# Four changed k pairs instead of three in the first feed-forward, and one k pair's low halves made by ScalarE and an accumulating DMA

## The chip, the core and the metric

The kernel runs on one core of one Trainium2 chip. The time is the device time of one execution in microseconds (us), the median of several runs. The engines of the core work side by side and wait for each other by semaphores: PE (TensorE, matrix products), PEld (its weight loads), DVE (VectorE), ACT (ScalarE), POOL (GpSimd) and SP (SyncE, which issues most of the transfers here). Transfers from HBM run on 16 shared DMA engines.

## The reference, cut to what is touched

The program computes two transformer blocks on 256 tokens of width 2048, in float32. The change is in the first block's feed-forward:

```
hn = rmsnorm(h, ffn_norm[l])                                  # 256 x 2048
h = h + (silu(hn @ w_gate[l]) * (hn @ w_up[l])) @ w_down[l]   # w_gate, w_up: 2048 x 5632
```

The two products hn @ w_gate and hn @ w_up are the ones whose schedule changes. What is computed stays as it is.

## The kernel before, in words

**Split operands.** A float32 operand is used as two parts, hi (the value rounded to the narrower matmul form, called F32R here) and lo (value minus hi). A product of two such operands is three matmuls: hi x hi, hi x lo, lo x hi (`product`, lines 1005 to 1007 are its three matmuls).

**Tiles and pairs.** The 5632 columns of w_gate and w_up are cut into 11 strips of 512 (W). A strip of w_gate and the same strip of w_up form one pair, f0 to f10 (`run_b[2:13]`); `ffn_b` is f1 to f10. The contraction over 2048 rows is cut into eight k pairs, 0 to 7. Each k pair has two chunks of 2 x 128 rows x 512 columns (512 KB): h = 0 from w_gate, h = 1 from w_up. Below, (k, h) is a chunk, so (7, 0) is k pair 7's chunk of w_gate.

**Plain and changed k pairs.** In a plain k pair (`plain_pair`) each chunk needs 4 products, so a k pair is 8 products or 24 matmuls. In a changed k pair (`strassen`, the Strassen-Winograd scheme on 2 x 2 blocks) it is 7 products or 21 matmuls. For that, DVE adds up four new tiles of 128 x 512 (`sums`, lines 2430, 2431, 2434, 2436): three go to the tile tf (sums T1, T2 and T4), the fourth replaces part of chunk h = 1 in place (T3). ACT makes their hi parts (`t_hi_of`, line 1608) and DVE their lo parts (`t_lo_of`, line 2450). tf has two sets in turn, so the sums of a changed k pair wait until PE is through with the changed k pair before the last one. Which k pairs are changed stands in the tuple F_S = (0, 3, 5). f0 has none (E_S).

**The activations' side.** A changed k pair also needs four combinations of the blocks of hn. They are built once, while f0 runs, for all later pairs: `x_forms` (DVE, lines 2401 to 2408/2409), `x_form_hi` (ACT, line 1580) and `x_form_lo` (DVE, line 2414). Those of the feed-forward are in xf, three places.

**A chunk's way.** There are six places for chunks (wf; wf_raw is the same memory read as plain float32; the second half of a place holds first the raw chunk and then its lo part). The k-th chunk takes the place of the chunk six before it. SP (`pair_chunks`, line 653) waits until PE has counted that chunk as used (f_used) and issues the load. Then ACT makes hi (`f_hi_of`, line 1601), then DVE makes lo in place (`f_lo_of`, line 2443), and PE waits for lo by the counter f_lo. In a changed k pair PE counts chunk 0 used after 6 matmuls and chunk 1 after 12, since it multiplies with the b21 and b22 parts early; only in k pair 0, where the result banks are still being read, it does that "late", after 15 and 18 matmuls.

**What sets the order.** Every engine's order is written out by hand. Within a pair f_n, ACT takes: the gates of the pair before (`gates_on`, line 1615), the hi parts and t_hi as listed, `p1_copy` (line 1651: copies one PSUM bank after the last changed k pair, k = 5, is done), the first three chunks and t_hi(0) of the next pair, `ff_copy`, and (1, 1) and (2, 0) of the next pair. DVE takes lo(1, 1), lo(2, 0), `gated_up` of the pair before (line 2505), lo(2, 1), the changed k pair 3, lo(4, 0), lo(4, 1), the changed k pair 5, the lo parts of k pairs 6 and 7, `middle` (lines 2465, 2467, 2468: combines PSUM banks, waits for p1_copy), and `to_next`: the first two sums of the next pair's k pair 0, `middle_end` (line 2473, counts y_ok), the other two sums, lo(0, 0), lo(0, 1), lo(1, 0), t_lo(0), then `finish` and `finish_up` (lines 2485, 2486, 2498), which read the result banks when PE is through with k pair 7. Ahead of k pair 7 PE waits for y_ok and turns the finished strip of the pair before (8 transposes, line 694).

**POOL** does nothing between its load of hres at 428 us and the one of gfbc at 1302 us.

Of the kernel before, what the change touches and what calls it, by code (L numbers as in the profile page):

```python
# [29 lines left out]
ALU = mybir.AluOpType  # L30
# [68 lines left out]
F_S = (0, 3, 5)  # L99
# [116 lines left out]
def two_blocks(nc, a, out):  # L216
    ctx = ExitStack()
    with ctx:
# [157 lines left out]
        t1_ok, t2_ok, t3_ok, t4_ok = sem("t1_ok"), sem("t2_ok"), sem("t3_ok"), sem("t4_ok")  # L376
        t_hi, t_lo, t_used = sem("t_hi"), sem("t_lo"), sem("t_used")
# [309 lines left out]
        def _(pe):  # L687
# [357 lines left out]
            def forms(p, k):  # L1045

                if p.wide:
                    return [[x_place(p.stage, F_S.index(k))[0][:, j, f, :] for j in range(2)] for f in range(4)]
                if p.run:
                    place = AGAIN_PLACE if p is e1 and k in E_AGAIN else D_S2.index(k)  # L1050
                    return [[ef4[:, place, j, f, :] for j in range(2)] for f in range(4)]
                return [operand(p, 2 * k, 1)] + [[ef[:, D_S.index(k), j, f, :] for j in range(2)] for f in range(3)]

            def strassen(p, k, begun):
# [12 lines left out]
                pe.wait_ge(f_lo, ca + 1)  # L1067
# [273 lines left out]
        def _(act):  # L1341
# [251 lines left out]
            def f_hi_of(p, k, h):  # L1593
# [497 lines left out]
        def _(dve):  # L2091
# [1093 lines left out]
        def _(pool):  # L3185
# [66 lines left out]

            pool.wait_ge(f_used, F_END)
# [57 lines left out]
```

## Time and profile before

| | us |
|---|---|
| median of 3 runs | 2432.6 (2431.69 to 2432.75) |
| span of the profiled execution | 2429.9 |
| PE busy in it | 2417.6 |
| DVE busy | 1881.4 |
| ACT busy | 1387.7 |
| POOL busy | 50.6 |

The span is the time from the first to the last instruction of one profiled execution; the run time also has what lies around it, 2.7 us by the median. PE's clock was granted in full except at the edges (mean 0.999). The pairs f1 to f10 lie between 643.8 and 1068.0 us of the span. The transfers' engines were busy 61 to 66% of the time. A row of the timeline gives an instruction's start, its duration, its engine, line and operands; matmul durations overlap, so their cost is the distance between starts.

### The profile page before, as it was taken

Reading aid. Unit: us, or ns where it says so; the run is one execution under the profiler, and the core shown is the slowest. Engines: PE = TensorE matmul, PEld = TensorE weight load, DVE = VectorE, ACT = ScalarE, POOL = GpSimd, SP = SyncE. Lnnn points to the kernel's source line nnn. Section 1 sums busy time; section 2 is a strip of 40 time slices with the busy share of each in tenths; the row PEclk is TensorE's granted clock in tenths of the full one; section 3 lists DMA queues with packets and bytes.
Section 4 is the critical chain, followed back from the end, with each engine's and each line's share of the span. In section 5 each row is a group of like instructions: output and inputs, shape, how many; then the busy total and the mean of one; then the engine's idle time right before and its main releaser. Section 6 shows DMA issues by size and latency. Waiting matters only on the chain.

```text
span 2429.9 us, 29002 instructions
## 1 busy us (share of the span) xinstructions
PE 2417.6 (99%) x11145; PEld 2008.2 (83%) x11145; DVE 1881.4 (77%) x2411; ACT 1387.7 (57%) x1744; POOL 50.6 (2%) x93
## 2 busy tenths in 40 slices
PE   9999999999999999999999999999999999999998
PEld 7888888888888888888888888888788888888887
DVE  6455555688898888989777587664889999999877
ACT  6446555445655555556456464564666666666554
POOL 1000110000000000000001100000000000000000
PEclk9999999999999999999999999999999999999999
DMA  7655555666666666666666555566566666666675
GB/s 238 198 172 155 185 156 162 217 192 191 191 197 200 201 195 203 195 192 202 197 208 198 167 154 161 155 191 197 167 197 193 196 200 188 194 195 189 200 215 169
DMA packets 239299, 460.11 MB, mean 189 GB/s; under 512 B 16582, under 2 KB 18800, under 8 KB 238528
## 3 DMA queue, kind: packets, MB, share of 16 engines
q1 hardware_dynamic: 237760, 452.65, 61.2%
q0 software_dynamic: 1376, 5.69, 0.7%
q8 instruction: 85, 1.39, 0.2%
q14 instruction: 46, 0.38, 0.1%
q10 hardware_dynamic: 32, 0.01, 0.0%
HBM read 456.19 MB, written 2.10 MB: 189 GB/s over the span
## 4 chain that ended last, share of the span: by engine, by line
PE 98%; DVE 1%; DMA 0%; SPq 0%; issue 0%; ACT 0%; DVEq 0%; ACTq 0%
PE acc L1005 16%; PE acc L1007 16%; PE acc L1006 16%; PE acc L721 11%; PE acc L723 11%; PE acc L722 11%; PE mis L1006 3%; PE mis L1005 3%; PE mis L1007 3%; PE mis L694 1%; PE mis L1290 1%; PE mis L819 1%; PE mis L1199 1%; PE acc L740 1%; PE acc L741 1%; PE acc L742 1%
## 5 line engine op out<-in xcount | busy, mean ns | idle before, releaser
L1601 ACT ACTIVATE wf<-wf_raw 128x1024 fp32r<-128x1024 f32 x544 | 568.4, 1058 | 548.3 <-DVE wf_raw L2431 219.1
L2443 DVE TENSOR_TENSOR wf<-wf_raw,wf 128x1024 fp32r<-128x1024 f32 x544 | 643.3, 1219 | 79.1 <-ACT wf L1601 75.6
L2099 DVE TENSOR_TENSOR lo<-raw,hi 128x1024 fp32r<-128x1024 f32 (+1 forms) x313 | 376.5, 1219 | 231.1 <-ACT hi L1354 228.7
L1354 ACT ACTIVATE hi<-raw 128x1024 fp32r<-128x1024 f32 (+1 forms) x313 | 321.0, 1049 | 162.9 <-PE acc L723 139.0
L1005 PE MATMUL acc<-wf,xb_hi 128*128 128x512 f32 x931 | 365.3, 392 | 0.0
L1007 PE MATMUL acc<-wf,xb_lo 128*128 128x512 f32 x931 | 362.7, 390 | 0.0
L1006 PE MATMUL acc<-wf,xb_hi 128*128 128x512 f32 x931 | 362.3, 389 | 0.0
L721 PE MATMUL acc<-hi,xa_hi 128*128 128x512 f32 (+1 forms) x576 | 224.4, 390 | 0.0
L723 PE MATMUL acc<-hi,xa_lo 128*128 128x512 f32 (+1 forms) x576 | 221.8, 385 | 0.0
L722 PE MATMUL acc<-lo,xa_hi 128*128 128x512 f32 (+1 forms) x576 | 221.6, 385 | 0.0
L721 PE MATMUL acc<-hi,xb_hi 128*128 128x512 f32 x544 | 216.4, 398 | 0.0
L723 PE MATMUL acc<-hi,xb_lo 128*128 128x512 f32 x544 | 212.2, 390 | 0.0
L722 PE MATMUL acc<-lo,xb_hi 128*128 128x512 f32 x544 | 211.9, 389 | 0.0
L1005 PE MATMUL acc<-wf,ff_top_hi 128*128 128x512 f32 x543 | 211.5, 390 | 0.0
L1007 PE MATMUL acc<-wf,ff_in_place_lo 128*128 128x512 f32 x543 | 211.3, 389 | 0.0
L1006 PE MATMUL acc<-wf,ff_top_hi 128*128 128x512 f32 x543 | 211.2, 389 | 0.0
L1007 PEld LDWEIGHTS acc<-wf,xb_lo 128*128 128x128 f32 x931 | 174.8, 188 | 36.6
L1005 PEld LDWEIGHTS acc<-wf,xb_hi 128*128 128x128 f32 x931 | 174.8, 188 | 35.7 <-DVE wf L2443 0.6
L1006 PEld LDWEIGHTS acc<-wf,xb_hi 128*128 128x128 f32 x931 | 174.9, 188 | 35.3
L723 PEld LDWEIGHTS acc<-hi,xa_lo 128*128 128x128 f32 x576 | 108.1, 188 | 21.5
L721 PEld LDWEIGHTS acc<-hi,xa_hi 128*128 128x128 f32 x576 | 108.2, 188 | 20.4
L722 PEld LDWEIGHTS acc<-lo,xa_hi 128*128 128x128 f32 x576 | 108.3, 188 | 20.3
(530 smaller groups left out, 3800.0 us busy)
## 6 DMA issues: line engine op xcount, KB each, us to landing
raw<-in_w_in SPq DMA_DIRECT2D x215, 512.0 KB, 4.2
wf_raw<-in_w_ffn_in SPq DMA_DIRECT2D x160, 512.0 KB, 3.7
wf_raw<-in_w_gate SPq DMA_DIRECT2D x88, 512.0 KB, 3.7
wf_raw<-in_w_up SPq DMA_DIRECT2D x88, 512.0 KB, 3.8
wf_raw<-in_w_down SPq DMA_DIRECT2D x88, 512.0 KB, 4.5
wf_raw<-in_w_ffn_out SPq DMA_DIRECT2D x88, 512.0 KB, 4.0
wf_raw<-in_w_out SPq DMA_DIRECT2D x32, 512.0 KB, 4.5
raw<-in_w_o SPq DMA_DIRECT2D x32, 512.0 KB, 4.9
```

What stands on the lines that cost most here:

```text
L694: last = nc.tensor.transpose(mis[pair][:, kb, t * P:(t + 1) * P], src[:, t, kb * P:(kb + 1) * P], ident[:, :])
L721: nc.tensor.matmul(o, xh, wh, start=kb == 0, stop=False)
L722: nc.tensor.matmul(o, xh, wl, start=False, stop=False)
L723: last = nc.tensor.matmul(o, xl, wh, start=False, stop=kb == k - 1)
L740: nc.tensor.matmul(o, xh, wh, start=kb == 0, stop=False)
L1005: nc.tensor.matmul(o, x[0], wh, start=first, stop=False)
L1006: nc.tensor.matmul(o, x[0], wl, start=False, stop=False)
L1007: return nc.tensor.matmul(o, x[1], wh, start=False, stop=end)
L1354: nc.scalar.activation(hi[:, slot, :, 0:width], raw[:, slot, :, 0:width], ACT.Copy)\
L1601: nc.scalar.activation(wf[:, f_slot[c], 0, :, :], wf_raw[:, f_slot[c], 1, :, :], ACT.Copy)\
L2099: V.tensor_tensor(lo[:, slot, :, 0:width], raw[:, slot, :, 0:width], hi[:, slot, :, 0:width].bitcast(F32), ALU.subtract).then_inc(lo_ready, 1)
L2443: V.tensor_tensor(wf[:, f_slot[c], 1, :, :], wf_raw[:, f_slot[c], 1, :, :], wf[:, f_slot[c], 0, :, :].bitcast(F32), ALU.subtract).then_inc ...
```

## The change

The table of changed k pairs becomes one table for each stage; the first feed-forward now has (0, 2, 4, 5) in place of (0, 3, 5), the other stages stay as they are. With four of them, a fourth combination of hn is built during f0, in the place xo, which the stage before has used. For k pair 7 of f1 to f10, DVE no longer makes the lo parts: ACT makes hi and then writes minus hi over it from the raw chunk, in place of the raw chunk; a DMA issued by POOL then loads the same chunk from HBM again and adds it to minus hi, which leaves lo. PE waits for that DMA (lo_in) instead of f_lo. POOL waits for minus_hi before each.

```diff
-F_S = (0, 3, 5)
+S_K = dict(out=(0, 3, 5), ffn=(0, 2, 4, 5), ffn2=(0, 3, 5))
+S_AT = dict(out=(3, 1, 2), ffn=(0, 3, 1, 2), ffn2=(0, 1, 2))
...
+N_K = 7
...
+        def by_dma(p, k):
+
+            return p in ffn_b and k == N_K
+
+        def lo_made(p, k, h):
+
+            c = p.chunk(k, h)
+            if by_dma(p, k):
+                return lo_in[h], 16 * (ffn_b.index(p) + 1)
+            return f_lo, c + 1 - sum(q.chunk(N_K, j) < c for q in ffn_b for j in range(2))
...
                 nc.scalar.activation(wf[:, f_slot[c], 0, :, :], wf_raw[:, f_slot[c], 1, :, :], ACT.Copy)\
                     .then_inc(f_hi, 1)
+                if by_dma(p, k):
+                    act.wait_ge(f_hi, c + 1)
+                    nc.scalar.activation(wf[:, f_slot[c], 1, :, :], wf_raw[:, f_slot[c], 1, :, :], ACT.Copy, scale=-1.0)\
+                        .then_inc(minus_hi, 1)
...
@@ ACT, f0
             f_hi_of(f0, 7, 0)
+            x_form_hi("ffn", 3)
             f_hi_of(f0, 7, 1)
@@ ACT, every pair of ffn_b
                 f_hi_of(p, 2, 1)
                 f_hi_of(p, 3, 0)
+                t_hi_of(p, 2)
                 f_hi_of(p, 3, 1)
                 f_hi_of(p, 4, 0)
-                t_hi_of(p, 3)
                 f_hi_of(p, 4, 1)
                 f_hi_of(p, 5, 0)
+                t_hi_of(p, 4)
                 f_hi_of(p, 5, 1)
                 f_hi_of(p, 6, 0)
                 t_hi_of(p, 5)
@@ DVE, f0
             x_form_lo("ffn", 2)
+            x_forms("ffn", 3)
             f_lo_of(f0, 7, 0)
             f_lo_of(f0, 7, 1)
+            x_form_lo("ffn", 3)
@@ DVE, every pair of ffn_b
                 f_lo_of(p, 1, 1)
-                f_lo_of(p, 2, 0)
+                strassen(p, 2)
                 gated_up(run_b[p.no - 1])
-                f_lo_of(p, 2, 1)
-                strassen(p, 3)
-                f_lo_of(p, 4, 0)
-                f_lo_of(p, 4, 1)
+                f_lo_of(p, 3, 0)
+                f_lo_of(p, 3, 1)
+                strassen(p, 4)
                 strassen(p, 5)
-                for k in (6, 7):
-                    f_lo_of(p, k, 0)
-                    f_lo_of(p, k, 1)
+                f_lo_of(p, 6, 0)
+                f_lo_of(p, 6, 1)
                 middle(p)
@@ POOL
+            for i, p in enumerate(ffn_b):
+                for h in range(2):
+                    c = p.chunk(N_K, h)
+                    pool.wait_ge(minus_hi, 2 * i + h + 1)
+                    if i:
+                        pool.wait_ge(lo_in[h], 16 * i)
+                    pool.dma_start(wf[:, f_slot[c], 1, :, :],
+                                   (w_gate, w_up)[h][:, CK * N_K:CK * N_K + CK, p.i * W:(p.i + 1) * W],
+                                   accum_op=ALU.add).then_inc(lo_in[h], 16)
```

ACT, pair f10, from the gates on, before. wf<-wf_raw is a hi part (f_in4 and the like name the place of its chunk: here (2, 1), (3, 0), (3, 1), (4, 0), then (4, 1)), tf<-tf_raw is t_hi.

```order
L1615 ACTIVATE dsum<-dsum,small 128x512
L1601 ACTIVATE wf<-wf_raw 128x1024 [waits f_in4]
L1601 ACTIVATE wf<-wf_raw 128x1024 [waits f_in1]
L1601 ACTIVATE wf<-wf_raw 128x1024 [waits t3_ok,f_in0]
L1601 ACTIVATE wf<-wf_raw 128x1024 [waits f_in3]
L1608 ACTIVATE tf<-tf_raw 128x1536 [waits t4_ok]
L1601 ACTIVATE wf<-wf_raw 128x1024 [waits f_in5]
```

The same place now, where the lines have moved (1601 is 1616, 1608 is 1627, 1615 is 1634):

```order
L1634 ACTIVATE dsum<-dsum,small 128x512
L1616 ACTIVATE wf<-wf_raw 128x1024 [waits t3_ok,f_in4]
L1616 ACTIVATE wf<-wf_raw 128x1024 [waits f_in1]
L1627 ACTIVATE tf<-tf_raw 128x1536 [waits t4_ok]
L1616 ACTIVATE wf<-wf_raw 128x1024 [waits f_in0]
L1616 ACTIVATE wf<-wf_raw 128x1024 [waits f_in3]
L1616 ACTIVATE wf<-wf_raw 128x1024 [waits t3_ok,f_in5]
```

The first t_hi of a pair is now that of k pair 2 and stands right behind hi(3, 0), whose chunk is loaded to place 1; in the form before, the first one belonged to k pair 3 and stood behind hi(4, 0).

ACT at the end of the same pair, before: t_hi(5), hi(6, 1), hi(7, 0), hi(7, 1), p1_copy.

```order
L1608 ACTIVATE tf<-tf_raw 128x1536 [waits t4_ok]
L1601 ACTIVATE wf<-wf_raw 128x1024 [waits f_in0]
L1601 ACTIVATE wf<-wf_raw 128x1024 [waits f_in3]
L1601 ACTIVATE wf<-wf_raw 128x1024 [waits f_in5]
L1651 ACTIVATE dsum<-mis 128x512 [waits staged,t_used]
```

And now:

```order
L1627 ACTIVATE tf<-tf_raw 128x1536 [waits t4_ok]
L1616 ACTIVATE wf<-wf_raw 128x1024 [waits f_in0]
L1616 ACTIVATE wf<-wf_raw 128x1024 [waits f_in3]
L1620 ACTIVATE wf<-wf_raw 128x1024 [waits f_hi]
L1616 ACTIVATE wf<-wf_raw 128x1024 [waits f_in5]
L1620 ACTIVATE wf<-wf_raw 128x1024 [waits f_hi]
L1670 ACTIVATE dsum<-mis 128x512 [waits staged,t_used]
```

Two more ACT instructions stand ahead of p1_copy, each behind a wait for the one before it.

DVE at the end of f0, before: lo(6, 1), the third x_form_lo, lo(7, 0) and lo(7, 1), then the first sum of f1.

```order
L2443 TENSOR_TENSOR wf<-wf_raw,wf 128x1024 [waits f_hi]
L2414 TENSOR_TENSOR xf<-xf_raw,xf 128x512 [waits xf_hi]
L2443 TENSOR_TENSOR wf<-wf_raw,wf 128x1024 [waits f_hi] x2
L2640 ISA x4
L2430 TENSOR_TENSOR tf_raw<-wf_raw 128x512 [waits t_used,f_in0,f_in1]
```

And now (2443 is 2464, 2414 is 2435, 2430 is 2451, 2401 to 2409 are 2422 to 2430):

```order
L2464 TENSOR_TENSOR wf<-wf_raw,wf 128x1024 [waits f_hi]
L2435 TENSOR_TENSOR xf<-xf_raw,xf 128x512 [waits xf_hi]
L2422 TENSOR_TENSOR usum<-xb_hi,xb_lo 128x512 [waits xf_sum]
L2427 TENSOR_TENSOR xf_raw<-usum 128x128 [waits dve_chain]
L2428 TENSOR_TENSOR xf_raw<-usum 128x128
L2429 TENSOR_TENSOR xf_raw<-usum,xf_raw 128x128 [waits dve_chain]
L2430 TENSOR_TENSOR xf_raw<-usum,xf_raw 128x128 [waits dve_chain]
L2464 TENSOR_TENSOR wf<-wf_raw,wf 128x1024 [waits f_hi] x2
L2435 TENSOR_TENSOR xf<-xf_raw,xf 128x512 [waits xf_hi]
L2663 ISA x4
L2451 TENSOR_TENSOR tf_raw<-wf_raw 128x512 [waits t_used,f_in0,f_in1]
```

Six instructions more stand between lo(6, 1) and the sums of f1.

## Rows read from the trace of the kernel before

**Rows 1.** The page: its head and its busy times by engine
```profile
span 2429.9 us, 29002 instructions
...
PE 2417.6 (99%) x11145; PEld 2008.2 (83%) x11145; DVE 1881.4 (77%) x2411; ACT 1387.7 (57%) x1744; POOL 50.6 (2%) x93
```

**Rows 2.** Table by stretches: one pair's period; busy us by engine, clock, DMA
```profile
949.60:991.90 42.30, 42.30 (x192) 35.12 (x192) 37.48 (x41) 23.68 (x24) 0.00 (x0) 1.00 0.65 199
```

**Rows 3.** Waits between 640 and 1080 us: total us, times, longest
```profile
PEld acc L1005 <- DVE usum L2495: 0.4, 1, 0.4
```

**Rows 4.** Timeline of PE in f8 and f9: start, us, what
```profile
966.65 0.39 PE L1005 MATMUL mis<-wf,xb_hi 128*128 128x512 f32 x1
...
976.86 1.04 PE L694 MATMUL mis<-ident,stg 128*128 128x128 f32 x8
...
983.18 0.39 PE L1005 MATMUL mis<-wf,xb_hi 128*128 128x512 f32 x1
```

**Rows 5.** Timeline of SP's queue, then the landing of the load at 969.6
```profile
969.56 0.37 SPq L653 DMA_DIRECT2D wf_raw<-in_w_up  x1
...
986.78 0.37 SPq L653 DMA_DIRECT2D wf_raw<-in_w_gate  x1
...
DMA to landing us min/median/max: 4.9/4.9/4.9
```

**Rows 6.** Timeline of ACT in f8 and f9, idle time before in brackets
```profile
965.26 1.04 ACT L1601 ACTIVATE wf<-wf_raw 128x1024 fp32r<-128x1024 f32 x1
...
971.61 0.60 ACT L1651 ACTIVATE dsum<-mis 128x512 f32<-128x512 f32 x1
...
990.56 1.06 ACT L1601 ACTIVATE wf<-wf_raw 128x1024 fp32r<-128x1024 f32 x1 [2.37 <-DMA wf_raw<-in_w_gate]
...
994.55 1.06 ACT L1601 ACTIVATE wf<-wf_raw 128x1024 fp32r<-128x1024 f32 x1 [0.19 <-DMA wf_raw<-in_w_gate]
995.52 1.47 ACT L1608 ACTIVATE tf<-tf_raw 128x1536 fp32r<-128x1536 f32 x1
```

**Rows 7.** Timeline of DVE in f8 and f9
```profile
960.58 0.69 DVE L2430 TENSOR_TENSOR tf_raw<-wf_raw 128x512 f32<-128x512 f32 x1 [1.81 <-issue]
...
963.24 2.36 DVE L2443 TENSOR_TENSOR wf<-wf_raw,wf 128x1024 fp32r<-128x1024 f32 x2
965.51 1.75 DVE L2450 TENSOR_TENSOR tf<-tf_raw,tf 128x1536 fp32r<-128x1536 f32 x1
967.18 3.49 DVE L2443 TENSOR_TENSOR wf<-wf_raw,wf 128x1024 fp32r<-128x1024 f32 x3
...
972.74 0.69 DVE L2465 TENSOR_TENSOR usum<-mis,dsum 128x512 f32<-128x512 f32 x1
...
975.86 0.68 DVE L2473 TENSOR_TENSOR usum<-mis,dsum 128x512 f32<-128x512 f32 x1
...
987.65 1.40 DVE L2505 SCALAR_TENSOR_TENSOR stg<-usum,small,dsum 128x512 f32<-128x512 f32 x2
988.98 1.21 DVE L2443 TENSOR_TENSOR wf<-wf_raw,wf 128x1024 fp32r<-128x1024 f32 x1
```

**Rows 8.** Timeline of DVE, then PE, where f0 ends and f1 begins
```profile
631.22 0.68 DVE L2401 TENSOR_TENSOR usum<-xb_hi,xb_lo 128x512 f32<-128x512 f32 x1
...
634.73 2.36 DVE L2443 TENSOR_TENSOR wf<-wf_raw,wf 128x1024 fp32r<-128x1024 f32 x2
...
643.15 1.75 DVE L2450 TENSOR_TENSOR tf<-tf_raw,tf 128x1536 fp32r<-128x1536 f32 x1
...
645.20 0.39 PE L1005 MATMUL mis<-tf,xf 128*128 128x512 f32 x1
```

**Rows 9.** Transfers by POOL: KB each, median us from issue to landing
```profile
hres<-in_x POOLq DMA_DIRECT2D x1, 2048.0 KB, 8.8
...
g2bc<-in_attn_post_norm POOLq DMA_DIRECT2D x1, 1024.0 KB, 5.0
...
walpha<-in_w_alpha_up POOLq DMA_DIRECT2D x1, 32.0 KB, 4.0
```

More of the change, by code:

```diff
@@ L107 @@
 O_S = (3, 5)
-X_ORDERS = ((0, 1, 2), (0, 1, 2), (0, 1, 2))
 E_S = ()
+N_K = 7
 FD, FE, FF_, FG = 0, 1, 2, 3
@@ L376, in two_blocks @@
         t1_ok, t2_ok, t3_ok, t4_ok = sem("t1_ok"), sem("t2_ok"), sem("t3_ok"), sem("t4_ok")
+        minus_hi = sem("minus_hi")
+        lo_in = [sem(f"lo_in{j}") for j in range(2)]
         t_hi, t_lo, t_used = sem("t_hi"), sem("t_lo"), sem("t_used")
@@ L499, in two_blocks @@
                 for i in range(first, dict(out=DT // 2, ffn=FT, ffn2=FT, down=DT // 2, down2=DT // 2)[stage]):
-                    nk, forms = KD // CK, F_S
+                    nk, forms = KD // CK, S_K.get(stage)
                     if stage in ("down", "down2"):
@@ L503, in two_blocks @@
                     elif i == first:
-                        forms = dict(out=O_S, ffn=E_S, ffn2=F_S[1:])[stage]
+                        forms = dict(out=O_S, ffn=E_S, ffn2=S_K["ffn2"][1:])[stage]
                     p = Pair(sum(map(len, runs)), run, stage, i, nk, forms, c, g, tile0)
@@ L536, in forms_due @@
         def forms_due(stage, q):
-            at = ("out", "ffn", "ffn2").index(stage)
-            return len(F_S) * at + X_ORDERS[at].index(q) + 1
+            before = ("out", "ffn", "ffn2").index(stage)
+            return sum(len(S_K[s]) for s in ("out", "ffn", "ffn2")[:before]) + q + 1
         def x_place(stage, q):
-            return (xo[:, 0], xo_raw[:, 0]) if stage == "out" and q == 0 else (xf[:, q], xf_raw[:, q])
+            j = S_AT[stage][q]
+            return (xo[:, 0], xo_raw[:, 0]) if j == 3 else (xf[:, j], xf_raw[:, j])
         def sums_of(p):
@@ L1047, in forms @@
                 if p.wide:
-                    return [[x_place(p.stage, F_S.index(k))[0][:, j, f, :] for j in range(2)] for f in range(4)]
+                    return [[x_place(p.stage, S_K[p.stage].index(k))[0][:, j, f, :] for j in range(2)] for f in range(4)]
                 if p.run:
@@ L1066, in strassen @@
                 a11, a12, a22 = operand(p, 2 * k, 0), operand(p, 2 * k + 1, 0), operand(p, 2 * k + 1, 1)
-                pe.wait_ge(f_lo, ca + 1)
+                pe.wait_ge(*lo_made(p, k, 0))
                 product(bank_p1, a11, *b11, touch(p, "p1", begun), end)
@@ L1070, in strassen @@
                     product(c11, a12, *b21, False, False).then_inc(f_used, 1)
-                pe.wait_ge(f_lo, cb + 1)
+                pe.wait_ge(*lo_made(p, k, 1))
                 if p.wide and p.i <= p.run + 1:
-                    pe.wait_ge(xf_lo, forms_due(p.stage, F_S.index(k)))
+                    pe.wait_ge(xf_lo, forms_due(p.stage, S_K[p.stage].index(k)))
                 if p is e1 and k in E_AGAIN:
@@ L1096, in plain_pair @@
                     outs = results_of(p)[h]
-                    pe.wait_ge(f_lo, c + 1)
+                    pe.wait_ge(*lo_made(p, k, h))
                     for kk in range(CK):
@@ L1329, in _ @@
                     if t == 0:
-                        pe.wait_ge(f_lo, c + 1)
+                        pe.wait_ge(*lo_made(e1, k, h))
                     for kk in range(CK):
@@ L2395, in x_forms @@
             def x_forms(stage, q):
-                k, x, n = F_S[q], xa if stage == "out" else xb, forms_due(stage, q)
+                k, x, n = S_K[stage][q], xa if stage == "out" else xb, forms_due(stage, q)
                 if n > 1:
```

## The prediction, made before the changed kernel had run

> **What bounds the kernel now.** First the page's busy times [rows 1]: PE is busy for 2417.6 of 2429.9 us. Then the stretch of the change, by stretches: one pair of the feed-forward takes 42.3 us, PE is busy all of it at the full clock, DVE for 37.5 and ACT for 23.7 [rows 2]. The waits between 640 and 1080 us name PE almost nowhere; the longest is 0.4 us, once [rows 3]. So the time here is the number of matmuls, and DVE is the next engine behind, with 4.8 us of a pair to spare. I take T for the moment PE begins a pair (983.18 for f9) [rows 4].
>
> A matmul costs the distance of starts. From 966.65 (first matmul of k pair 5) to 976.86 (transposes) PE does 21 + 24 = 45 matmuls in 10.21 us [rows 4]: 0.227 us each. A changed k pair is 4.76 us, a plain one 5.44, the transposes with what follows them 0.88 (976.86 to 983.18 less 5.44). The profiled execution lasts 2429.9 us and the median is 2432.6, so 2.7 us lie outside the span and stay; the sum is made on the span.
>
> **What it removes.** In each of f1 to f10 one k pair goes from 24 matmuls to 21: 30 x 0.227 = 6.8 us less. That is the whole gain there can be, 0.28%. DVE loses two lo parts a pair and gains four sums and a t_lo.
>
> **f0, once: +2.4 us.** The fourth set of combinations stands in DVE's row ahead of the sums of f1. From 631.22 to 634.73 DVE does one such set, one lo part and the x_form_lo in 3.51 us; less one lo part (2.36 - 1.22 = 1.14) that is 2.37 [rows 7, 8]. Nothing idles from there to t_lo(0) of f1, which ends at 643.15 + 1.75 = 644.90, and PE wants it at 645.20 [rows 8]. It would come at 647.27: PE waits 2.1 us there, and with the copies behind it, which held PE up already [rows 3], the shift is the full 2.37. Bounds: 0 (if DVE made it up elsewhere, which I don't see) and 2.4.
>
> **DVE's row inside a pair: +5.2 us.** Without waits PE would begin k pair 2 at T + 10.2, k pair 4 at T + 20.4, k pair 5 at T + 25.2. When does DVE get there? The sums of k pair 2 need chunk (2, 1), whose place PE frees at T; a load takes 990.56 - 986.78 = 3.8 us until its reader starts [rows 5, 6], so they begin at about T + 4.0. Sums and two lo parts take 965.51 - 960.58 = 4.93 us [rows 7]: T + 8.9. But t_lo(2) needs t_hi(2), and ACT has hi(3, 0) ahead of that. That chunk is loaded only after PE's late release in k pair 0, at 986.78 = T + 3.6 [rows 5], and ACT starts on it at 990.56 = T + 7.38; the next one starts 995.52 - 994.55 = 0.97 later and lasts 1.47 [rows 6]. So t_hi(2) ends at T + 9.82, and DVE has lost 1.0 us. From there nothing stops it: t_lo 1.67 (967.18 - 965.51), gated_up 1.33 (988.98 - 987.65), two lo parts 2.27 (965.51 - 963.24), the whole changed k pair 4 in 967.18 - 960.58 = 6.60 [rows 7]: 9.86 + 1.67 + 1.33 + 2.27 + 6.60 = T + 21.73. The sums of k pair 5 take 2.66 and lo(5, 0) 1.21 [rows 7]: it is there at T + 25.60, 0.43 us after PE wants it. t_lo(5) ends at 21.73 + 4.93 + 1.75 = 28.41; PE, now later by 0.43, wants it at 28.33: 0.08 more. That is 0.5 us a pair, 5.2 us in ten. The pair's sums then wait for the next pair's loads again, so the delay does not add up from pair to pair. What makes this so close: DVE's work in a pair goes from 37.5 to about 37.5 - 2.3 + 2.65 + 1.67 = 39.5 us of a period of 42.
>
> **p1_copy: +1 us.** ACT starts hi(6, 1) at 965.26, 4.68 us after the first sum of k pair 5 [rows 6, 7]; from T + 21.73 that is T + 26.41. Then hi(7, 0) at 27.37, minus hi after it (it waits for it: 1.15) at 28.52, hi(7, 1) at 29.48, minus hi at 30.63, p1_copy at 31.6, 0.60 long [rows 6], about 1 us after PE has ended k pair 5 (30.6). From middle to y_ok DVE needs 975.86 + 0.68 - 972.74 = 3.80 [rows 7]: T + 36.0, and PE ends k pair 6 at 25.6 + 4.8 + 5.4 = 35.9. So 0.1 us a pair, 1 in ten; DVE has room for it because two lo parts are gone from ahead of middle.
>
> **The accumulating DMA: no cost, if it lands within 7.2 us.** POOL gets minus hi (7, 0) at T + 29.6 and (7, 1) at T + 31.7; PE wants the lo parts at 35.9 + 0.88 = T + 36.8 and T + 39.5. The budgets are 7.2 and 7.8 us from issue to landing. No accumulating transfer is in this trace. The nearest rows are POOL's plain ones: 4.0 us for 32 KB, 5.0 for 1 MB, 8.8 for 2 MB beside other loads [rows 9]. The new one fetches 512 KB and must read and write 512 KB of the tile; by amount it stands next to the 1 MB row, with other loads beside it. I take 6.5 us, the ends are 4.0 and 8.8. At 8.8 PE waits 1.6 us in each pair, +16.
>
> The Trainium skill, DMA: Bandwidth & Descriptors, section Anatomy of one DMA — SWDGE (gpsimd) path, gives 2.0 us and the bytes over 436 GB/s for such a transfer, 3.2 us here; by that the DMA is hidden with 4 us to spare and the sum is unchanged. Its row nearest here, 1 MB, would be 4.4 us by the rule and took 5.0 [rows 9], so the trace is slower than the rule.
>
> **Sum:** 2429.9 - 6.8 + 2.4 + 5.2 + 1.0 = 2431.7 for the span, and 2434.4 us for the median (+0.07%): the matmuls saved come back as waits for DVE.
>
> **Rivals.**
>
> (A) The accumulating DMA is late. For it: it reads the tile as well as HBM, so it may hold the DMA engines for twice as long as a load, they already are busy 65% of a pair [rows 2], the second is issued 2.1 us behind the first, and the next pair's loads come in between. It decides from 7.2 us for the first or 7.8 for the second; each us beyond that costs 10 us in ten pairs. At 8.2 us the kernel is slower: about 2434.4 + 9 = 2443; at 8.8, 2450; if the second queues fully behind the first, 2 us more a pair, up to 2470. Against it: 1 MB landed in 5.0. An unknown operation with 0.7 to 1.3 us between my value and the budget, and a price of 10 us for each us: more than a third. The Trainium skill, Collectives: The Full Stack, section The bandwidth ceiling: the fold count and why AG ≠ RS ≠ AR, says that an add in the DMA path takes two source reads and halves the rate; nothing in this trace shows such an add. By that rule the transfer would end near the end of its budget.
>
> (B) The load of (0, 1) of the next pair is late. It is issued 969.56 - 966.65 = 2.91 us into k pair 5 and lands 4.9 later [rows 4, 5]: T + 33.4. DVE wants it at T + 34.1, in the middle of what y_ok needs. The first accumulating DMA starts at 29.6 beside it. If it takes half the engines from it for 1.5 us, the load is 0.8 late and PE waits for y_ok: +0.1 to +0.8 a pair, 2435 to 2442.
>
> (C) DVE keeps up: the load of (3, 0) or the wait on PE's side is kinder by 0.4 us. Then only f0's cost remains: 2432.6 - 6.8 + 2.4 = 2428.2. Against it: the numbers of the chain repeat from pair to pair.
>
> That 30 matmuls don't go away can't be: the order of PE has 30 rows fewer.
>
> **How the numbers follow.** A measurement tells about 0.2% (4.9 us) from no change: faster is below 2427.7, slower above 2437.5. The forecast has 0.42, all in "same". A has 0.38 (0.35 slower, 0.03 same), B 0.12 (0.08 slower, 0.04 same), C 0.08 (0.03 faster, 0.05 same). Faster 0.03, same 0.54, slower 0.43. The range leaves out C's lower half and the upper part of A, where both transfers queue: 2429.5 to 2456. The likeliest case's own range is 2431 to 2437, from a stall by DVE of 0.3 to 0.8 us a pair and p1_copy's 0 to 0.1.
>
> **What would show it.** A period of 42.2 us a pair (42.3 - 0.68 + 0.6); PE waiting at k pair 5 for line 2464 (lo) by about 0.4 us and for the transposes (line 694's successor) by about 0.1; DVE idle 1 us ahead of t_lo(2) for ACT; one PE wait of about 2 us at f1's k pair 0 for t_lo; no PE wait for POOL's DMA, which lands in 5 to 7 us. I am wrong if PE waits at k pair 7 for the landing (A), if DVE waits for a load ahead of the next pair's sums (B), or if PE does not wait at k pair 5 at all (C).

## The result, and the profile after

| | before | after |
|---|---|---|
| median | 2432.7 us (4 runs) | 2458.6 us (3 runs, 2456.5 to 2459.9) |
| ratio | | 1.0107, 95% interval 1.0091 to 1.0122 |
| span of the profiled execution | 2429.9 us | 2454.8 us |

The changed kernel is slower by 1.1%: 26.0 us by the medians, 24.9 us by the spans. The prediction was 2434.4 us with a range of 2429.5 to 2456: the time is above the range. A fourth run of the changed kernel took 7581 us; its cause is not known, it did not come again, and no number here includes it.

The page of the changed kernel, parts 1 and 3 (busy us, share, instructions; DMA queue: packets, MB, share of 16 engines):

```profile
span 2454.8 us, 29078 instructions
...
PE 2426.8 (99%) x11115; PEld 1999.8 (81%) x11115; DVE 1904.3 (78%) x2447; ACT 1415.2 (58%) x1775; POOL 74.7 (3%) x113
...
q1 hardware_dynamic: 237760, 452.65, 59.8%
q0 software_dynamic: 6816, 16.17, 3.2%
```

Against [rows 1] PE has 30 matmuls fewer and yet the span is longer. The share of busy time hardly shows the loss; the waits do. Waits between 600 and 1100 us (engine, line, waited for: total us, times, longest):

```profile
PEld acc L1020 <- DMA wf<-in_w_up: 11.4, 10, 1.4
PEld mis L1020 <- DVE tf L2471: 9.6, 20, 2.3
...
PEld acc L1020 <- DMA wf<-in_w_gate: 6.2, 7, 1.5
...
PEld acc L1020 <- DVE usum L2519: 4.3, 9, 0.5
PEld mis L1020 <- DVE wf L2464: 4.2, 12, 0.6
...
PEld mis L709 <- DVE usum L2494: 1.0, 5, 0.2
```

Before, the one such row was 0.4 us [rows 3]. The largest item is k pair 7 waiting for the accumulating DMA, 17 times in ten pairs. These are waits of the weight loads, which run ahead of the matmuls; what the matmuls lose is less in sum, and is worked out below. The same in one pair, in PE's weight loads (f5 into f6; in brackets the idle time before and what ended it):

```profile
894.21 0.19 PEld L1020 LDWEIGHTS mis<-wf,xb_hi 128*128 128x128 f32 x1 [0.36 <-DVE wf L2464]
897.01 0.19 PEld L1020 LDWEIGHTS mis<-tf,xf 128*128 128x128 f32 x1 [0.19 <-DVE tf L2471]
904.56 0.86 PEld L709 LDWEIGHTS mis<-ident,stg 128*128 128x128 f32 x8 [0.21 <-DVE usum L2494]
906.58 0.19 PEld L1020 LDWEIGHTS acc<-wf,xb_hi 128*128 128x128 f32 x1 [1.16 <-DMA wf<-in_w_gate]
910.51 0.19 PEld L1020 LDWEIGHTS acc<-wf,xb_hi 128*128 128x128 f32 x1 [1.33 <-DMA wf<-in_w_up]
914.96 0.19 PEld L1020 LDWEIGHTS mis<-tf,xf 128*128 128x128 f32 x1 [0.50 <-DVE tf L2471]
917.36 0.19 PEld L1020 LDWEIGHTS acc<-wf,xf 128*128 128x128 f32 x1 [0.48 <-DVE usum L2519]
```

Read it from the top. Lo(5, 0) is late by 0.36 us and t_lo(5) by 0.19: the prediction's stall by DVE. The weight load waits 0.21 for y_ok: p1_copy. Then the two landings, 1.16 and 1.33 us. The last two rows belong to the next pair and were not predicted: t_lo(0) and finish_up are late as well.

What PE itself loses can be worked out from its own rows: the distance between matmul starts less 0.227 us each, and less 0.88 us for the transposes, summed by place. The mean of the nine periods (44.49 us, against a floor of 41.69) comes out as 1.7 us at the two landings, 0.85 us in k pair 0 of the next pair, 0.25 us at k pair 5, and nothing at the transposes. So about 60% of a pair's 2.8 us is the landings and 30% the knock-on in the next pair. Why the next pair is late, ACT and DVE show (their timelines, same notation):

```profile
910.68 1.06 ACT L1616 ACTIVATE wf<-wf_raw 128x1024 fp32r<-128x1024 f32 x1 [5.62 <-DMA wf_raw<-in_w_gate]
```
```profile
911.77 1.23 DVE L2464 TENSOR_TENSOR wf<-wf_raw,wf 128x1024 fp32r<-128x1024 f32 x1 [3.55 <-ACT wf L1616]
```

ACT stands idle for 5.6 us for chunk (1, 0) of the next pair, and DVE for 3.6 behind it. That load is issued at 902.09, between the two POOL issues and their landings, and takes 8.6 us. POOL's queue and the page's list of its transfers (KB each, median us to landing):

```profile
898.34 1.20 POOL L3280 DMA_DIRECT2D wf<-in_w_gate  x1 [41.92 <-ACT wf L1620]
900.38 1.20 POOL L3280 DMA_DIRECT2D wf<-in_w_up  x1 [0.83 <-ACT wf L1620]
```
```profile
wf<-in_w_gate POOLq DMA_DIRECT2D x10, 512.0 KB, 7.5
...
wf<-in_w_up POOLq DMA_DIRECT2D x10, 512.0 KB, 9.1
```

And stretches of one us, the first before the first add has begun to move data (last two columns: share of the 16 DMA engines that is busy, GB/s):

```profile
898.00:899.00 1.00, 1.00 (x6) 0.80 (x6) 1.00 (x2) 0.99 (x2) 0.66 (x1) 1.00 0.95 367
...
902.00:903.00 1.00, 1.00 (x6) 0.84 (x5) 0.99 (x3) 0.00 (x0) 0.00 (x0) 1.00 1.05 178
903.00:904.00 1.00, 1.00 (x6) 0.81 (x5) 1.00 (x3) 0.00 (x0) 0.00 (x0) 1.00 1.14 203
904.00:905.00 1.00, 1.00 (x8) 0.75 (x7) 1.00 (x2) 1.00 (x1) 0.00 (x0) 1.00 1.12 203
```

The DMA engines are full and yet move 178 to 203 GB/s; with loads alone, as full, they move 367. By queue (q0 is POOL's, q1 has the loads; packets, MB, share of the 16 engines), in the stretches 903 to 904, then 908 to 909, then 909 to 910:

```profile
q0 software_dynamic: 105, 0.20, 114.3%
```
```profile
q1 hardware_dynamic: 196, 0.38, 98.3%
q0 software_dynamic: 9, 0.01, 5.7%
```
```profile
q1 hardware_dynamic: 95, 0.17, 43.7%
q0 software_dynamic: 4, 0.01, 4.4%
```

From 902 to 905 the loads move 11 packets against 294 of the adds, so the load issued at 902.09 all but stands still until the adds thin out. How long an add holds them: q0's share is 3.2% in place of 0.7% for 20 transfers more, (0.032 - 0.007) x 2454.8 / 20 = 3.1 us of all 16 engines for 512 KB. A plain load takes 0.598 x 2454.8 / 863 = 1.70 us (452.65 MB are 863 times 512 KB). The ratio is 1.8; by e4's share below, 3.4 us, it is 2.0.

The Trainium skill, Collectives: The Full Stack, section The bandwidth ceiling: the fold count and why AG ≠ RS ≠ AR, says of a ReduceScatter that its add needs two source reads and so has half the rate of a copy: for this DMA within one core the trace agrees, 1.8 to 2.0. By the fit of the Trainium skill, DMA: Bandwidth & Descriptors, section Anatomy of one DMA — SWDGE (gpsimd) path, an estimate for 512 KB is 3.2 us: the measured 7.5 and 9.1, and 6.1 for an add alone, decide against it here.

### The profile page after: what moved, and what is told of

Its sections match the earlier page's. It is cut to its first block, busy times and chain, and to the rows that moved or that the text cites. A ratio compares the mean times of both kernels' runs of the same rounds, so it can differ in the third digit from the quotient of the medians.

```text
span 2454.8 us, 29078 instructions
## 1 busy us (share of the span) xinstructions
PE 2426.8 (99%) x11115; PEld 1999.8 (81%) x11115; DVE 1904.3 (78%) x2447; ACT 1415.2 (58%) x1775; POOL 74.7 (3%) x113
## 3 DMA queue, kind: packets, MB, share of 16 engines
q1 hardware_dynamic: 237760, 452.65, 59.8%
## 4 chain that ended last, share of the span: by engine, by line
PE 88%; DMA 4%; DVE 4%; ACT 2%; issue 0%; DVEq 0%; SPq 0%; ACTq 0%
PE acc L1020 14%; PE acc L1022 14%; PE acc L1021 14%; PE acc L736 10%; PE acc L738 10%; PE acc L737 10%; PE mis L1020 3%; PE mis L1022 3%; PE mis L1021 3%; DMA wf_raw<-in_w_gate 2%; DMA wf<-in_w_up 1%; DVE wf L2464 1%; ACT wf L1616 1%; DVE tf L2471 1%; DMA wf_raw<-in_w_up 1%; PE mis L1305 1%
## 5 line engine op out<-in xcount | busy, mean ns | idle before, releaser
L2464 DVE TENSOR_TENSOR wf<-wf_raw,wf 128x1024 fp32r<-128x1024 f32 x524 | 621.1, 1220 | 94.9 <-ACT wf L1616 90.7
L1020 PE MATMUL acc<-wf,xb_hi 128*128 128x512 f32 x861 | 339.9, 395 | 11.7 <-DMA wf<-in_w_up 7.2
L1022 PE MATMUL acc<-wf,xb_lo 128*128 128x512 f32 x861 | 335.6, 390 | 0.0
L1021 PE MATMUL acc<-wf,xb_hi 128*128 128x512 f32 x861 | 335.3, 389 | 0.0
L1020 PEld LDWEIGHTS acc<-wf,xb_hi 128*128 128x128 f32 x861 | 161.8, 188 | 50.5 <-DMA wf<-in_w_up 11.4
L1022 PEld LDWEIGHTS acc<-wf,xb_lo 128*128 128x128 f32 x861 | 161.6, 188 | 34.5
L1021 PEld LDWEIGHTS acc<-wf,xb_hi 128*128 128x128 f32 x861 | 161.9, 188 | 32.5
L2471 DVE TENSOR_TENSOR tf<-tf_raw,tf 128x1536 fp32r<-128x1536 f32 x74 | 129.7, 1753 | 4.6 <-ACT tf L1627 3.8
```

Source lines behind the costliest of these rows:

```text
L1020: nc.tensor.matmul(o, x[0], wh, start=first, stop=False)
L1021: nc.tensor.matmul(o, x[0], wl, start=False, stop=False)
L1022: return nc.tensor.matmul(o, x[1], wh, start=False, stop=end)
L2464: V.tensor_tensor(wf[:, f_slot[c], 1, :, :], wf_raw[:, f_slot[c], 1, :, :], wf[:, f_slot[c], 0, :, :].bitcast(F32), ALU.subtract).then_inc ...
L2471: V.tensor_tensor(tt[:, 1, :, :], tr[:, 1, :, :], tt[:, 0, :, :].bitcast(F32), ALU.subtract)\
```

## The experiments

Each experiment is the changed kernel with a switch for which halves of k pair 7 go by DMA (BY_DMA), and the edit shown. "Period" is the distance from one pair's transposes to the next pair's in the trace, the mean of nine; a floor follows from 42.37 before, less 3 x 0.227: 41.69 us. Times of the kernel before stood at 2432.5 to 2432.6 us in all of them.

| kernel | changed k pairs | k pair 7 | median us | ratio, 95% interval | period us |
|---|---|---|---|---|---|
| before | 3 | DVE | 2432.6 | | 42.37 |
| after | 4 | 2 adds | 2458.6 | 1.0091 to 1.0122 | 44.49 |
| e1_forms_only | 4 | DVE | 2443.3 | 1.0028 to 1.0061 | 43.08 |
| e2_dma_only | 3 | 2 adds | 2459.2 | 1.0095 to 1.0129 | 44.65 |
| e3_plain_dma | 4 | 2 copies | 2437.0 | 1.0007 to 1.0026 | 42.46 |
| e4_one_dma | 4 | 1 add | 2436.0 | 1.0006 to 1.0025 | 42.38 |
| e5_gate_first | 4 | 1 add | 2434.5 | 0.9998 to 1.0017 | 42.17 |
| e6_one_dma_f0 | 4 | 1 add | 2436.4 | 1.0007 to 1.0026 | 42.54 |
| e7_gate_f0 | 4 | 1 add | 2433.7 | 0.9995 to 1.0013 | 42.39 |
| e8_three_plain | 3 | 2 copies | 2435.6 | 1.0005 to 1.0024 | 42.73 |
| e9_three_one_dma | 3 | 1 add | 2438.9 | 1.0018 to 1.0038 | 43.06 |
| e10_both_gate | 4 | 2 adds | 2456.0 | 1.0082 to 1.0115 | 44.57 |
| e11_p1_first | 3 | 1 add | 2458.5 | 1.0087 to 1.0120 | 45.00 |

The two kernels with copies, e3 and e8, leave out the subtraction of hi for k pair 7.

### One part alone: e1 and e2

```diff
 e1
+BY_DMA = ()
...
                 f_lo_of(p, 6, 1)
+                f_lo_of(p, 7, 0)
+                f_lo_of(p, 7, 1)
                 middle(p)
```
```diff
 e2, and the order on ACT and DVE of the kernel before
-S_K = dict(out=(0, 3, 5), ffn=(0, 2, 4, 5), ffn2=(0, 3, 5))
+S_K = dict(out=(0, 3, 5), ffn=(0, 3, 5), ffn2=(0, 3, 5))
```

> Four changed k pairs as in the changed kernel, but k pair 7's two lo parts are made by DVE again, ahead of middle; POOL does nothing between f0 and f10. Theory 1 (the accumulating DMA costs the time; the four changed k pairs cost little): without it the pair is bound by DVE's row, 0.4 us at k pair 5 as before, and middle comes 2.3 us later, so that PE waits for y_ok by 0.5 to 1.0 us a pair. Period 42.5 to 43.0 us against 44.5, f0 the same 2.4 us once: 2432.7 + 10 x (42.8 - 42.3) + 2.4 = 2440, between 2437 and 2443. Rival (the four changed k pairs, by DVE's row and the late t_lo(0) and finish_up, cost the time, and the DMA is only where the waits are put down): the period stays over 44 us, the time over 2455. No PE wait for in_w_gate or in_w_up.

> The kernel before's three changed k pairs (0, 3, 5) with their order on ACT and DVE and without the fourth set in f0; k pair 7's lo parts by minus hi and the accumulating DMA. Theory 1: the DMA is late with three changed k pairs too, and the loads of the next pair with it; period 44 to 45.8 us, the time between 2450 and 2467, slower than the kernel before by 0.7 to 1.4%, with PE waits for in_w_gate and in_w_up as in the changed kernel. Rival (it is the four changed k pairs that push the DMA's issue late): with the lighter row the minus hi comes earlier, the DMA is hidden, and the time is 2430 to 2434.

Theory 1 has it in both: e2's 2459.2 us lies in its range, e1's 2443.3 us and period of 43.08 us just above theirs (2437 to 2443, 42.5 to 43.0), and the rivals' numbers are far off. Without the DMA the four changed k pairs cost 10.7 us, bound by DVE (busy 414 of 430 us between 640 and 1070, against 381 before). With the DMA and the old three k pairs the whole loss is there. The rival, that a heavier DVE row pushes the DMA late, falls. The two costs don't add up to the changed kernel's, 10.7 and 26.6 against 26.0 us: there the adds take work from DVE (busy 384 of the 430), which is what e1 lacks. e2's waits between 600 and 1100 us:

```profile
PEld acc L1021 <- DMA wf<-in_w_up: 10.8, 10, 1.7
...
PEld mis L710 <- DVE usum L2493: 7.4, 9, 1.0
```

### The add, or the issue by POOL: e3 and e8

```diff
 e3 (e8: the same on e2)
-                                   (w_gate, w_up)[h][:, CK * N_K:CK * N_K + CK, p.i * W:(p.i + 1) * W],
-                                   accum_op=ALU.add).then_inc(lo_in[h], 16)
+                                   (w_gate, w_up)[h][:, CK * N_K:CK * N_K + CK, p.i * W:(p.i + 1) * W]).then_inc(lo_in[h], 16)
```

> The changed kernel, but POOL's DMA copies the chunk in place of adding it: the same issues, waits and 512 KB from HBM, no add and no read of the tile. It leaves out the subtraction for k pair 7, whose lo parts are then the raw chunk. Theory 1 (the add holds the DMA engines 1.8 times as long as a load, 3.07 us against 1.70 for 512 KB): POOL's rows fall from 7.5 and 9.1 us to about 5 and 5.5, they are hidden, the next pair's loads land in under 5 us, the period is 42.0 to 42.2 us: 2432.7 - 2.5 + 2.4 = 2432.6, between 2430 and 2435. Rival 2 (a DMA issued by POOL is slow to begin, whatever it does): POOL's rows stay at 7 to 9 us and the time stays over 2450.

> e2 (three changed k pairs, both chunks of k pair 7 by minus hi and POOL's DMA), but the DMA copies in place of adding. It leaves out the subtraction for k pair 7, whose lo parts are the raw chunk. Theory (of e2's 2.3 us a pair the add makes the larger part, and the two minus hi ahead of p1_copy on ACT, which make y_ok late as in e9, the rest): PE waits for y_ok only, 0.5 to 1.2 us a pair, none for in_w_gate or in_w_up; period 43.0 to 43.5 against 44.65, 2438 to 2444. Rival (the minus hi and the issue on POOL cost it all): over 2452.

The same issues, waits and bytes from HBM, without the add: 2.0 us of a period go (44.49 to 42.46; with three changed k pairs 44.65 to 42.73). No PE wait for POOL's DMA is left in either. e3's transfers and queue between 640 and 1080 us, then those of the changed kernel:

```profile
q0 software_dynamic: 5440, 10.49, 7.9%
...
wf<-in_w_gate POOLq DMA_DIRECT2D x10, 512.0 KB, 5.3
wf<-in_w_up POOLq DMA_DIRECT2D x10, 512.0 KB, 4.7
```
```profile
q0 software_dynamic: 4896, 9.44, 12.4%
...
wf<-in_w_up POOLq DMA_DIRECT2D x9, 512.0 KB, 9.2
```

20 copies hold the engines 0.079 x 440 / 20 = 1.74 us each, as a load does. The 4896 packets of the second page are 18 adds at 272 packets each: 0.124 x 440 / 18 = 3.0 us each. In e8 the copies land in 5.9 and 6.5 us (median). So it is the add and no slow start by POOL. e8 came out 2.4 us better than the lower end expected: its y_ok wait is 0.6 us a pair in the weight loads, as expected, but the period is only 0.36 us longer than before. e3 is 2 us above its range. Its trace has two reasons: the stall by DVE that e4 shows next, and a fall of the clock, told under f0 below.

### One add in place of two: e4 and e9

```diff
 e4 (e9: the same on e2)
+BY_DMA = (1,)
...
                 f_lo_of(p, 6, 1)
+                f_lo_of(p, 7, 0)
                 middle(p)
```

> The changed kernel, but only chunk (7, 1) goes by minus hi and the accumulating DMA; (7, 0)'s lo part is DVE's again, ahead of middle. Theory 1 (the second queues behind the first, and together they take the DMA engines from the next pair's loads for 6 us): one alone lands in 6.5 to 7.5 us, inside its budget of 7.8 or 8.8, the next loads lose 1 to 2 us and nobody waits for that; period 42.0 to 42.3: 2432, between 2430 and 2435. Rival (one accumulating DMA beside two loads is late all the same): PE waits 0.5 to 1.5 us a pair for in_w_up, 2438 to 2448.

> The kernel before's three changed k pairs with its order, and only (7, 1) by minus hi and the accumulating DMA. It is e2 with one DMA in place of two. Theory (one transfer lands in about 6.1 us as in e4, inside its budget of 7.7, and only two in a row are late): nothing changes against the kernel before, 2432.6, between 2431 and 2435. Rival (with three changed k pairs the loads of k pair 0 and 1 of the next pair meet it and it is late by 0.6 us, middle and y_ok by 0.2): 2438 to 2441.

e4's only add lands in 6.1 us, and PE never waits for it: 22.6 us of 26.0 are gone. Its DMA list, and the waits that are left in one of its pairs:

```profile
wf<-in_w_up POOLq DMA_DIRECT2D x10, 512.0 KB, 6.1
```
```profile
884.25 0.19 PEld L1021 LDWEIGHTS mis<-wf,xb_hi 128*128 128x128 f32 x1 [0.83 <-DVE wf L2465]
887.05 0.19 PEld L1021 LDWEIGHTS mis<-tf,xf 128*128 128x128 f32 x1 [0.21 <-DVE tf L2472]
```

That is the predicted stall by DVE at k pair 5, and it alone eats the 0.68 us that a pair saves: period 42.38 against 42.37. The time, 2436.0, is 1 us over the range expected. Part of it is the stall, put at 0.5 us and 0.69 by the period less the floor. But the trace is of the fastest of ten executions, 2433.9 us, which lies in the range; what makes the others up to 4.4 us longer is in no trace. In e9 the add lands in 6.1 too and isn't waited for, but y_ok (0.5 us a pair), finish_up and t_lo(0) are late: 2438.9, the rival's number. So even one add isn't free where the row behind it has no slack: e9 with no matmul saved is slower than before by 0.28%.

### What is left in e4: e5, e6 and e7

```diff
 e5, ACT
                 gates_on(run_b[p.no - 1])
+                f_hi_of(p, 2, 0)
                 f_hi_of(p, 2, 1)
...
-                f_hi_of(after, 2, 0)
 e5, DVE
-                strassen(p, 2)
                 gated_up(run_b[p.no - 1])
+                strassen(p, 2)
```
In e6 ACT's hi parts of the combinations follow the same order.

```diff
 e6, DVE in f0
+            x_forms("ffn", 2)
             norm4(2, ss_h4, ss_h, rs_h, SQ["h"])
+            x_form_lo("ffn", 2)
             f_lo_of(f0, 6, 0)
-            x_forms("ffn", 2)
+            x_forms("ffn", 3)
             f_lo_of(f0, 6, 1)
-            x_form_lo("ffn", 2)
-            x_forms("ffn", 3)
+            x_form_lo("ffn", 3)
             f_lo_of(f0, 7, 0)
             f_lo_of(f0, 7, 1)
-            x_form_lo("ffn", 3)
```

> As e4 (one accumulating DMA, for (7, 1)), and in each pair ACT takes the gates ahead of hi(2, 0), and DVE takes gated_up ahead of the sums of k pair 2, into the 1.06 us that it idles there for the load of (2, 1) in e4. Theory (what e4 loses in a pair is DVE's row from that load to k pair 5, 0.8 us of weight-load wait or 0.4 us of PE's own): the sums of k pair 2 begin about 0.3 us later instead of gated_up standing 1.4 us behind them, so the row reaches k pair 5 about 1.0 us earlier; no PE wait is left in a pair, the period falls from 42.4 to 42.0 us or a little below: 2436.0 - 4 = 2432, between 2430 and 2434. Rival (PE's loss per pair in e4 is no wait for DVE): the time stays at 2435 to 2437.

> As e4, and in f0 the third and the fourth set of combinations are built one place earlier each, so that the fourth no longer stands between the last lo parts of f0 and f1's first sums. Theory (the fourth set costs 2.4 us once, as predicted): PE's wait of 2.3 us for t_lo(0) at f1's k pair 0 shrinks to under 0.5: 2436.0 - 2.2 = 2433.8, between 2432.5 and 2435. Rival (the work is only moved: PE waits in f0's k pairs 6 and 7 instead): no change, 2436.

> Both edits of e5 and e6 together, on e4. Theory: the gains add, 2436.0 - 4 - 2.2 = 2429.8, between 2427.5 and 2432, a little faster than the kernel before (2432.6): 30 matmuls (6.8 us) less what is left of the waits. Rival (one of the two only moves its wait): 2432 to 2434.

e5: six of the nine periods fall to 41.7 to 42.0 us, the floor or close to it; PE's wait for lo(5, 0) is gone in those. One is 44.05: there the load of (1, 0), issued at 847.67, lands in 6.4 us, and the add beside it in 7.6 instead of 6.2 (median); t_lo(0) is 0.79 us late and lo(5, 0) 1.38. Its rows in PE's weight loads:

```profile
858.41 0.19 PEld L1021 LDWEIGHTS mis<-tf,xf 128*128 128x128 f32 x1 [0.79 <-DVE tf L2473]
...
883.82 0.19 PEld L1021 LDWEIGHTS mis<-wf,xb_hi 128*128 128x128 f32 x1 [1.38 <-DVE wf L2466]
```

So the mechanism is shown in the trace; the gain is about 1.5 us of the 4 expected, and the time, 2434.5, is above the range. DVE is busy for 414 of the 430 us between 640 and 1070, so it passes a late load on. e6 went the rival's way: the wait for t_lo(0) of f1 shrank from 2.28 to 1.30 us only, and a new one stands in f0's k pair 6, where lo(6, 0) is now late (PE, then DVE):

```profile
635.16 0.47 PE L1021 MATMUL acc<-wf,xb_hi 128*128 128x512 f32 x1 [1.32 <-DVE wf L2465]
```
```profile
632.84 0.17 DVE L2130 RECIPROCAL small<-small 128x2 f32<-128x2 f32 x1 [1.94 <-ACT small L1375]
633.04 0.69 DVE L2436 TENSOR_TENSOR xf<-xf_raw,xf 128x512 fp32r<-128x512 f32 x1
633.79 1.22 DVE L2465 TENSOR_TENSOR wf<-wf_raw,wf 128x1024 fp32r<-128x1024 f32 x1
```

But this order makes DVE stand idle for 1.94 us for ACT, inside norm4, just ahead of that lo part; in the changed kernel it stood 0.27 us there. So e6 shows that this placing gains nothing, not that none would. e7, both edits, came out at 2433.7 us, in the rival's range and not the theory's, and is within its interval the same as e5 and as the kernel before. No version here beats the kernel before by what a measurement can tell.

### The same two adds with more slack on DVE, and an add issued later: e10 and e11

e10 is the changed kernel with e5's edit.

```diff
 e11, on e9: ACT
-                for k, h in ((6, 1), (7, 0), (7, 1)):
-                    f_hi_of(p, k, h)
-
+                f_hi_of(p, 6, 1)
+                f_hi_of(p, 7, 0)
                 p1_copy(p)
+                f_hi_of(p, 7, 1)
```

> The changed kernel (four changed k pairs, two accumulating DMAs) with e5's order: the gates ahead of hi(2, 0) on ACT, gated_up ahead of the sums of k pair 2 on DVE. Theory (the late landing sets the pair's end, so what DVE gains in the pair is not seen at its end): PE's waits for wf and tf at k pair 5 go, those for in_w_gate and in_w_up grow by as much; period 44.0 to 44.5, 2455 to 2459. Rival (the lateness starts in DVE's row, and an earlier minus hi brings the landing forward by as much as PE comes earlier, with the next pair's t_lo(0) and finish_up no longer late): period under 43.2, under 2443.

> e9 (three changed k pairs, one accumulating DMA) with p1_copy ahead of hi(7, 1) on ACT. In e9 p1_copy stands behind hi(7, 1), which waits 1.7 us for its load, and behind minus hi, and DVE idles 2.5 us for it ahead of middle. Theory (e9's 0.7 us a pair is this wait, y_ok, and not the DMA): p1_copy comes 2 to 3 us earlier, PE's wait for y_ok goes, the DMA is issued 0.6 us later and is hidden still: period 42.4, 2432.6 to 2434.5. Rival (the DMA's hold on the loads costs it): 2438 to 2440 as e9.

e10's time is the theory's, 2456.0 us, its period 44.57 just above it (44.0 to 44.5), and the rival (under 2443) falls. The way is only half as told. Between 600 and 1100 us the wait for in_w_up grows from 11.4 to 12.9, but in_w_gate's falls from 6.2 to 3.6, and those for tf and wf hardly move, 9.6 to 8.3 and 4.2 to 4.0. At k pair 5 six of the ten pairs have no wait for lo(5, 0) left, where in the changed kernel each had 0.2 to 0.6 us; in the other four it is 0.4 to 1.1 us. So the reordering gives 2.6 us by the medians with two adds, which the intervals don't separate from nothing, and the landing sets the end with it too; what makes those four late I haven't settled.

e11 was meant to free y_ok and missed: it is 24 us above the theory's range and 18.5 above the rival's. y_ok is nearly free (0.8 us in all, from 4.8 in e9), but p1_copy waits for PE to end k pair 5, which I had overlooked, and the hi part and minus hi of (7, 1) stand behind it. Its ACT, POOL and PE rows:

```profile
899.89 0.60 ACT L1671 ACTIVATE dsum<-mis 128x512 f32<-128x512 f32 x1 [2.84 <-PE acc L1023]
```
```profile
902.84 1.20 POOL L3281 DMA_DIRECT2D wf<-in_w_up  x1 [43.08 <-ACT wf L1621]
```
```profile
910.70 0.19 PEld L1021 LDWEIGHTS acc<-wf,xb_hi 128*128 128x128 f32 x1 [2.13 <-DMA wf<-in_w_up]
```

PE wants the chunk at 910.70 - 2.13 = 908.57, 5.7 us after the issue, and the add takes 7.8 us (median) beside the next pair's loads, the first of which is issued at 902.61. In e9 the budget is 7.7 and the landing 6.1. It wasn't planned so, but it tests the budget with a single add: 7.8 against 5.7 is 2.1 us late, and in the matmuls' starts the pairs lose 2.2 us there. The period grows by 1.9 us (43.06 to 45.00), less than that, since e9's waits for y_ok are gone. And a single add issued into the loads is as slow to land as the first of two.

## Why the prediction was wrong

**The matmuls, 6.8 us: right.** The floor of 41.7 us shows in most of e5's periods.

**f0, 2.4 us: right in place, too low.** PE's weight load waits 2.28 us for t_lo(0) at f1's k pair 0, at 648.05. By the matmuls' starts that k pair loses 2.9 us more than before in e4, and 4.3 in the changed kernel. "Nothing idles from there" did not hold: DVE stands 0.52 us for ACT's hi part of (7, 1) at 638.36, behind the new x_form_hi. The rest is a cost that the prediction didn't have. Behind the wait the granted clock falls to 0.50, the lower (1.2 GHz) of its two levels, and the matmuls start 0.43 us apart in place of 0.23 for about 3 us (PE's rows, then the stretch 649 to 650, the clock third from the end):

```profile
648.05 0.79 PE L1020 MATMUL mis<-tf,xf 128*128 128x512 f32 x1 [1.84 <-DVE tf L2471]
...
649.50 0.63 PE L1020 MATMUL mis<-tf,xf 128*128 128x512 f32 x1
649.92 0.63 PE L1021 MATMUL mis<-tf,xf 128*128 128x512 f32 x1
```
```profile
649.00:650.00 1.00, 1.00 (x4) 0.73 (x3) 1.00 (x3) 0.77 (x2) 0.00 (x0) 0.50 0.00 0
```

That costs about 1.5 us. It is in the profiled executions of the changed kernel, e1 and e3; in e4, e5 and e10 PE waits as long at the same place and the clock does not fall. In e11 it falls twice, behind waits for the add. What decides it, these traces don't show.

**DVE's row, 0.5 us a pair: right in place.** In the weight loads 0.36 and 0.19 us in the pair shown of after, 0.83 and 0.21 in e4; in the matmuls' starts 0.25 us a pair in after and 0.66 in e4. That the late landings give DVE time to catch up in after fits this, but is not tested. The way to it was not the one told: ahead of t_lo(2) DVE waits for ACT by 0.19 us, at 878.41, not 1.0. Instead the sums of k pair 2 begin later in e4, at 905.65, 4.6 us after the pair's first matmul at 901.03, not 4.0: the load of (2, 1), issued at 901.23, takes 4.3 us, not 3.8. The add isn't the cause, as it has landed at 895.3, and e1 without any has 4.1 us there. Two errors of opposite sign.

**p1_copy, 0.1 us a pair: nothing was lost by it.** The weight loads wait 0.2 us in five of the pairs, 1.0 us in all, but the transposes start no later behind the matmuls than before.

**The accumulating DMA: the step that failed.** The budgets were right: the first is issued at 898.34 and wanted at 906.58 - 1.16 = 905.42, 7.1 us against 7.2 worked out; the second, issued at 900.38, is wanted at 909.18, 8.8 us, which is the 7.8 worked out and the first's lateness. The landing was not: I took 6.5 us for each, by amount next to the 1 MB row [rows 9], and so put the DMA at nothing in the sum; the two landed in 7.5 and 9.1 us (median), and PE lost 1.7 us a pair to them. One add alone takes 6.1 in e4, so as the price of one it was right. Two of them, 2 us apart, are not two times one alone. The pair shown takes 12.2 us from the first issue at 898.34 to the second landing at 910.5. By queue and stretches of one us that is nearly 2 us before the first packet of an add, then 9 us, from 900 to 909, in which the engines are full with 6.0 us of the two adds and 3.3 us of loads, then 1.5 us in which they are half idle and the last five packets of the add go through. So the hold explains most of it, not the last 1.5 us. Rival A named the hold and the queue and had 0.38, and its upper part, to 2470, is where the time lies; the range left it out. A sum of holds could have been made from [rows 2] and A's own words; that it would have given the landing is not shown. Instead the value came from a row with few other transfers beside it.

**The knock-on: not in any rival.** B looked at (0, 1) of the next pair, which was hardly late. The next one, (1, 0), is issued at 902.09 into the full engines, lands after 8.6 us, and makes t_lo(0) and finish_up late by 0.5 us each in PE's weight loads, 0.85 us a pair in the matmuls' starts. The prediction held that a pair's delay does not add up to the next one's; it had only the stall by DVE in mind.

With one add, e4, the profiled span is 2432.1 us, where the sum had said 2431.7 for both; the second add brings 22.7 us more. That the sum met e4 so closely is luck in part: p1_copy costs nothing there, the stall by DVE and f0 cost more, and the execution is the fastest of ten. The 2.7 us that the sum added for what lies outside the span were such a mixture too: the runs have about 1.8 us there, and the rest is that the profiled execution was the fastest. Two slips of its sums, which nothing hangs on: by its own terms PE ends k pair 5 at T + 30.4, not 30.6, and rival A's time for a landing of 8.2 us is 2444, not 2443.

## What to carry to other kernels

Before a transfer is added, add up what every transfer in its window holds of the DMA engines, an accumulating one as two, and set the sum, with the 2 us that an add took here to its first packet, against the time to the last reader. No run tested this sum as a forecast. A landing time from a quiet place is the price of one alone. And look at what the loads issued behind it feed: here 0.85 of a pair's 2.8 us arose there. And waits of the weight loads overstate the loss in sum: what PE loses is read from the distance between its matmuls' starts. Work taken from a busy engine this way isn't free: e9 gives DVE 1.1 us a pair back and is slower.

## What the runs showed of the hardware

- An accumulating DMA of 512 KB into SBUF, issued by POOL, holds the 16 DMA engines for 3.0 to 3.4 us (after; e4: 0.077 x 440 / 10), a plain copy of the same by POOL 1.74 (e3) to 1.87 (e8: 0.085 x 440 / 20), a load 1.70.
- It lands in 6.1 us as the only one of its pair in e4 and e9 (5.8 to 6.8 in e4, 5.8 to 7.4 in e9), in 7.5 and 9.1 as two in a row, in 7.8 when issued among loads (e11); the plain copies in 5.3 and 4.7 in e3, in 5.9 and 6.5 in e8. The issue on POOL takes 1.20 us with the add and 0.71 without.
- While adds are under way the DMA engines are full at 178 to 203 GB/s, against 367 GB/s with loads alone.
- The load of (1, 0), on another queue, takes 8.6 us beside two adds and 4.7 beside one (e4, issued at 892.14). For scale, a load takes 3.8 to its reader before [rows 5, 6].
- A wait of PE of 1.84 us was followed by about 3 us at the lower clock level (a granted clock of 0.50) in the changed kernel, and by no fall in e4.
